# Gated linear attention in a three-part float32 kernel: products on halves of TensorE's array, and another order of VectorE's splits and norms

## The chip, the cores and the metric

The kernel runs on one core of a Trainium2 chip, in one launch. The metric is the device time of that launch in microseconds; the median of three runs of the kernel before is 2018.16 us (2017.99 to 2021.58). TensorE multiplies (PE in the profile, with its weight loads as PEld), VectorE (DVE) and ScalarE (ACT) work on what lies in the on-chip memory SBUF and empty TensorE's banks (PSUM, eight banks `ps` of 512 columns by 128 partitions), GpSimd (POOL) does a few elementwise products, SyncE (SP) issues the DMAs.

## The reference

Input is one sequence of 512 rows by 1024, in float32. Three blocks follow one another: gated linear attention with an MLP, windowed attention with sinks and an MLP, and a block of convolution, dilated attention and a gated feed-forward. The change is mostly in the first:

```python
def gla_mixer(h, w_in, w_gate_up, b_gate_up, g_norm, w_out):
    q, k, v, g, glr = jnp.split(h @ w_in, ...)          # 512, 512, 1024, 1024, 16 columns
    log_a = jax.nn.log_sigmoid(glr @ w_gate_up + b_gate_up) / 16
    # eight chunks of 64 rows, four heads: k 128 wide, v 256 wide
    bc = jnp.cumsum(log_a over a chunk)
    q_dec, k_inv, k_end = q * 128**-0.5 * exp(bc), k * exp(-bc), k * exp(b_last - bc)
    att = tril(q_dec @ k_inv.T)                          # 64 x 64 a chunk and head
    o_intra = att @ v
    dS = k_end.T @ v                                     # 128 x 256 a chunk and head
    S[n + 1] = S[n] * exp(b_last) + dS[n]                # over the chunks
    o = o_intra + q_dec @ S[n]
    o = rms_norm(o over 256, g_norm) * silu(g)
    return o @ w_out
```

Around it: `x = x + rms_norm(m)` and `h = rms_norm(x)` ahead of each MLP.

## The kernel before, in words

Every large matrix product is done in three fp32r products of split operands: high part times high part, high times low, low times high. A weight unit is 1024 columns by 128 partitions (512 KB). SyncE fetches it to one of four raw buffers `WR` (`fetch`, in one order through the kernel), ScalarE copies it rounded to `WH` (`a_cut`), VectorE subtracts to get the low part `WL` (`v_cut`); each of these waits for the buffer's last reader. `product` (L386 to L388) multiplies one unit with 512 columns of activations (`HH`, `HL`), 24 matmuls to a bank; `tokens` (L415 to L417) makes 128 rows of output from up to four units, two banks at a time. Products within an attention are in plain float32. Each engine runs its own list, written out by hand, in order; semaphores marked by name (`k.mark`, `k.on`) tie them, and `k.free[b]` names what frees bank b. `k.ring` sets the banks that products take in turn.

The gated linear attention, TensorE's list in `t_gla`:

- the normed rows are transposed (`t_turn`, L437), then nine projection units `gla_in`: the low-rank tile first (its 16 columns of weights padded to 128), then four of K and four of Q. `t_starts` does the first four, by halves of the rows, while later rows are still being normed. Evacuations are VectorE's (`evac`). After the sixth unit the low-rank result `GLR` (its row 32 is ones, for the bias) is multiplied with `WGU` (L600);
- eight products for V (`tokens`, p = 0 to 7; V's second half is added on VectorE by `evac_v`), and between them the cumulative sums of each head (`decays`, L517) and the transposition of the decayed K (`turn_k`, L526). ScalarE and VectorE work each head's exponentials in `decays(h)`;
- eight gate units `gla_g`, with the attention between them: `scores` (L535) of 128 rows and four heads to bank 3, which VectorE masks to `DG` with a block-diagonal mask; `intra` (L547) for two chunks in one product of 128 x 128; then chunk by chunk `chunk(n)`: the inter-chunk product with the state (L560, 64 columns), and the new state's product (L569, on 64 rows of the array, banks 7 and 4), which VectorE adds to the decayed state `ST` (L1732). ScalarE takes the output of two chunks from banks 5 and 6 (`outs`);
- the norm: squares by ScalarE, sums by TensorE with a matrix of ones (`o_sums`, L583; rows 0 to 255 after the sixth gate unit, both through bank 3), logarithm and exponential by ScalarE (`o_norm`), eight scalings by VectorE (L1742), times the gates on GpSimd (L2167), and `o_cut` splits the result to `HH`, `HL` (L1098, L1748), which the gate units have read until then;
- the output product `t_ends`, row tile by row tile, with the second half's sums between its first two parts. `a_ends` and `v_ends` then make mean, scale, sum, mean and normed row `MT` for each row tile, which `t_turn` transposes for the MLP.

The windowed attention (`t_swa`) runs eight pairs of heads: `score` (L682, each head on 64 rows of the array), `turn` (transposed weights, L697), `out` (product with V, L711), with projection units between, and `ahead` does parts of the output product for row tile 0 in the last two pairs. Its tail has its own order on VectorE (`early=True` in `v_ends`).

## Time and profile before

| what | us |
|---|---|
| median of three runs | 2018.16 |
| the profiled execution | 2019.09 |
| its span | 2017.3 |
| TensorE busy (matmul) | 1987.8 |
| TensorE weight loads | 1638.9 |
| VectorE busy | 1187.9 |
| ScalarE busy | 853.9 |
| GpSimd busy | 28.4 |

The span is that of the core's first to last instruction. A matmul in float32 stands in the trace as two records, one in fp32r as one. Matmuls are pipelined, so a record's duration is longer than the distance to the next record's start; prices are best read from start to start. Of the chain that ended last, TensorE holds 92%. All of the gated linear attention lies in the first 264 us of the span, the windowed attention with its tail between 589 and 779 us.

### The profile page before, as it was taken

How to read it: one execution, taken by the hardware profiler on the slowest of the kernel's cores; microseconds unless marked ns; L12 is line 12 of the kernel's file. 1: busy time of each engine (PE TensorE's matmuls, PEld its weight loads, DVE VectorE, ACT ScalarE, POOL GpSimd, SP SyncE). 2: the span in 40 equal slices, each digit the busy share in tenths (PEclk: the TensorE clock that was granted, in tenths of full speed). 3: DMA queues.
4: the chain of work that ended last, by engine and by line, in shares of the span. 5: the costliest groups of instructions: out<-in, count | busy, mean ns of one | idle time of the engine just before them, and what ended most of it. 6: DMA issues, size and time to landing. Idle time of an engine off the chain costs nothing.

```text
span 2017.3 us, 25047 instructions
## 1 busy us (share of the span) xinstructions
PE 1987.8 (99%) x9784; PEld 1638.9 (81%) x9784; DVE 1187.9 (59%) x1776; ACT 853.9 (42%) x1374; POOL 28.4 (1%) x34
## 2 busy tenths in 40 slices
PE   7999999999999999999999999999999999999999
PEld 7788898888888778888888987667788888888887
DVE  4344564444456756444445686777798647774764
ACT  4533544233335744423233426667634324442431
POOL 0001100000000000000000000000000000000000
PEclk9999999999999999999999999999999999999999
DMA  5131123223323113322323232222232313222321
GB/s 193 53 125 42 63 94 103 96 84 127 98 89 147 53 53 93 96 96 92 125 89 99 95 95 94 84 77 81 74 97 86 126 68 104 96 95 84 115 94 63
DMA packets 51857, 188.53 MB, mean 93 GB/s; under 512 B 5755, under 2 KB 6011, under 8 KB 51100
## 3 DMA queue, kind: packets, MB, share of 16 engines
q1 hardware_dynamic: 51740, 186.92, 28.1%
q8 instruction: 79, 1.29, 0.3%
q14 instruction: 38, 0.31, 0.1%
HBM read 184.80 MB, written 2.10 MB: 93 GB/s over the span
## 4 chain that ended last, share of the span: by engine, by line
PE 92%; DVE 3%; ACT 3%; issue 1%; DMA 0%; SPq 0%; DVEq 0%; ACTq 0%
PE ps L386 18%; PE ps L388 18%; PE ps L387 17%; PE ps L415 10%; PE ps L417 10%; PE ps L416 10%; DVE WL L1566 1%; PE ps L813 1%; PE ps L437 1%; PE ps L785 1%; PE ps L799 1%; PE ps L569 1%; PE ps L560 1%; PE ps L711 1%; PE ps L763 1%
## 5 line engine op out<-in xcount | busy, mean ns | idle before, releaser
L386 PE MATMUL ps<-HH,WH 128*128 128x512 f32 (+1 forms) x1784 | 667.2, 374 | 3.0 <-DVE HL L1593 1.7
L388 PE MATMUL ps<-HH,WL 128*128 128x512 f32 (+1 forms) x1784 | 655.5, 367 | 0.0
L387 PE MATMUL ps<-HL,WH 128*128 128x512 f32 (+1 forms) x1784 | 655.0, 367 | 0.0
L954 ACT ACTIVATE WH<-WR 128x1024 fp32r<-128x1024 f32 x305 | 320.6, 1058 | 622.8 <-PE ps L388 347.5
L1566 DVE TENSOR_TENSOR WL<-WR,WH 128x1024 fp32r<-128x1024 f32 x305 | 372.5, 1226 | 196.8 <-ACT WH L954 190.1
L386 PEld LDWEIGHTS ps<-HH,WH 128*128 128x128 f32 x1784 | 337.3, 189 | 71.9 <-issue 16.1
L388 PEld LDWEIGHTS ps<-HH,WL 128*128 128x128 f32 x1784 | 337.1, 189 | 55.8
L387 PEld LDWEIGHTS ps<-HL,WH 128*128 128x128 f32 x1784 | 337.7, 189 | 54.1 <-issue 1.9
L415 PE MATMUL ps<-WH,HIDH 128*128 128x512 f32 x624 | 243.4, 390 | 0.0
L417 PE MATMUL ps<-WL,HIDH 128*128 128x512 f32 x624 | 243.1, 390 | 0.0
L416 PE MATMUL ps<-WH,HIDL 128*128 128x512 f32 x624 | 243.0, 389 | 0.0
L1919 DVE SCALAR_TENSOR_TENSOR M<-AP,PAR,M 128x512 f32<-128x512 f32 x240 | 167.2, 757 | 0.3 <-ACT M L1274 0.3
L415 PEld LDWEIGHTS ps<-WH,HIDH 128*128 128x128 f32 x624 | 117.2, 188 | 24.8 <-DVE WL L1566 0.6
L416 PEld LDWEIGHTS ps<-WH,HIDL 128*128 128x128 f32 x624 | 117.2, 188 | 24.2
L417 PEld LDWEIGHTS ps<-WL,HIDH 128*128 128x128 f32 x624 | 117.2, 188 | 24.2
L1605 DVE TENSOR_TENSOR MT<-ps,MT 128x1024 f32<-128x1024 f32 x52 | 63.6, 1222 | 114.0 <-PE ps L417 114.0
L1815 DVE TENSOR_TENSOR HIDL<-RT,HIDH 128x512 fp32r<-128x512 f32 x64 | 44.3, 693 | 87.2 <-ACT HIDH L1164 87.2
L1160 ACT ACTIVATE RT<-RT 128x512 f32<-128x512 f32 x64 | 40.5, 632 | 121.1 <-DVE RT L1813 121.1
L2120 DVE COPY UP<-ps 128x512 f32<-128x512 f32 x44 | 30.4, 692 | 67.1 <-PE ps L388 67.1
L2133 DVE TENSOR_TENSOR X<-ps,X 128x1024 f32<-128x1024 f32 x24 | 29.4, 1223 | 53.0 <-PE ps L417 53.0
L415 PE MATMUL ps<-WH,HH 128*128 128x512 f32 x128 | 51.6, 403 | 1.2 <-DVE WL L1566 1.2
L1593 DVE TENSOR_TENSOR HL<-ps,HH 128x512 fp32r<-128x512 f32 x48 | 30.9, 685 | 33.6 <-ACT HH L974 33.6
(227 smaller groups left out, 2075.1 us busy)
## 6 DMA issues: line engine op xcount, KB each, us to landing
WR<-in_up SPq DMA_DIRECT2D x108, 512.0 KB, 3.6
WR<-in_down SPq DMA_DIRECT2D x86, 512.0 KB, 3.5
WR<-in_in SPq DMA_DIRECT2D x56, 512.0 KB, 3.6
WR<-in_swa_in SPq DMA_DIRECT2D x10, 512.0 KB, 4.3
WR<-in_gla_in SPq DMA_DIRECT2D x9, 512.0 KB, 6.6
WR<-in_gla_v SPq DMA_DIRECT2D x8, 512.0 KB, 3.5
WR<-in_gla_g SPq DMA_DIRECT2D x8, 512.0 KB, 4.7
GAIN<-in_gain SPq DMA_DIRECT2D x4, 1024.0 KB, 7.1
```

What stands on the lines that cost most here:

```text
L386: e.matmul(ps, wh, hi[:, c, cols], start=c == 0, stop=False)
L387: e.matmul(ps, wh, lo[:, c, cols], start=False, stop=False)
L388: y = e.matmul(ps, wl, hi[:, c, cols], start=False, stop=c == x.n - 1)
L415: e.matmul(m.ps[b + f], xh, x.wh[:, w], start=first, stop=False)
L416: e.matmul(m.ps[b + f], xl, x.wh[:, w], start=False, stop=False)
L417: y = e.matmul(m.ps[b + f], xh, x.wl[:, w], start=False, stop=last)
L954: e.activation(x.wh[:, 0:n], m.WR[:, u % RAW, 0:n], AF.Copy).then_inc(*k.mark("whi", u))
L1160: e.activation(buf, buf, AF.Square).then_inc(*k.mark("sqr", u))
L1566: e.tensor_tensor(x.wl[:, 0:n], m.WR[:, u % RAW, 0:n], x.wh[:, 0:n].bitcast(F32), A.subtract).then_inc(*k.mark("wlo", u))
L1605: e.tensor_tensor(out, p, out, A.add).then_inc(*k.mark("mv", *key))
L1815: e.tensor_tensor(m.HIDL[:, i % 16, :], buf, m.HIDH[:, i % 16, :].bitcast(F32), A.subtract).then_inc(*k.mark("hid", layer, i))
L1919: e.scalar_tensor_tensor(m.M[:, c, :], m.AP[:, c, t:t + T], par(m, "conv_w", c * 31 + t, 1), m.M[:, c, :], A.mult, A.add).then_inc(*k.mark ...
```

## The change

- Low-rank tile: it moves behind the four units of K. Its low weights are written by VectorE into columns 32 to 47 of each slice of the high ones, so that two products in place of three give both parts, in rows 0 to 15 and 32 to 47; `GLR` has 64 rows, `WGU` holds its weights twice, and the bias comes by adding a column of the identity.
- Scores: all four pairs of chunks at once, after the first gate unit, each chunk and head as 64 x 64 on one half of the array's columns, to banks 2 and 3; two maskings by VectorE into `ATT` (which lies where `BC` was, so the DMA of the gains waits for the last `intra`).
- `intra` chunk by chunk on the two halves of the array's rows, chunk 2t to bank 5 and 2t + 1 to bank 6; `states` for both chunks of a pair together, on row halves, to banks 2, 3 and 4, 7; `inter` alone. ScalarE takes each chunk's output (`outs(n)`). The last gate unit is cut after five of eight slices, and the last pair's work stands in the gap.
- The norm: VectorE adds the squares in pairs, sums are one product of 512 columns a pair of heads, in two banks; the first half's scaling moves to the eighth gate unit's step and stands ahead of the last state update on VectorE.
- The low part of the first gate unit is made within the last head's `decays`. V's products take their banks in the other order, gate units use two banks.
- Windowed attention: the first scores come after half a projection unit; `ahead` does three slices, then one. In its tail VectorE norms row tile 1 before it splits tile 0, and one weight split goes behind the evacuation of row tile 3. In the last block's `evac_y` a weight split moves ahead of the low part.

The diff, cut to what is spoken of:

```diff
-    m.GLR = over("GLR", [33, T], gains)
-    m.WGU = over("WGU", [33, T], gains + 2 * KB)
+    m.GLR = over("GLR", [64, T], gains)
+    m.WGU = over("WGU", [64, T], gains + 2 * KB)
     m.BC = over("BC", [128, 2, T], gains + 4 * KB)
+    m.ATT = over("ATT", [128, 4, 4, 64], gains + 4 * KB)
+GLA_O = (5, 6)
+GLA_DS = ((2, 3), (4, 7))
@@ t_gla
+    def low_rank(j):
+        x, b = k.units[u + j], k.bank()
+        e.wait_ge(*k.on("wlo", u + j))
+        e.wait_ge(*k.on(*k.free[b]))
+        for c in range(8):
+            w = x.wh[:, c * 128:(c + 1) * 128]
+            e.matmul(ps[b], w, hi[:, c, :], start=c == 0, stop=False)
+            y = e.matmul(ps[b], w, lo[:, c, :], start=False, stop=c == 7)
+        y.then_inc(*k.mark("unit", u + j))
+        k.free[b] = ("ev", u + j)
+        k.value["bank", u + j] = b
+    def scores():
+        for t in range(4):
+            b = 2 + t // 2
+            if t % 2 == 0:
+                e.wait_ge(*k.on(*k.free[b]))
+            for h in range(4):
+                f = (t % 2 * 4 + h) * 64
+                for s in range(2):
+                    sl = slice(t * 128 + 64 * s, t * 128 + 64 * s + 64)
+                    x = e.matmul(ps[b][64 * s:64 * s + 64, f:f + 64], m.KI[:, h, sl], m.Q[:, h, sl], start=True,
+                                 stop=True)
+            if t % 2:
+                x.then_inc(*k.mark("att", t // 2))
+                k.free[b] = ("mask", t // 2)
+        e.wait_ge(*k.on("mask", t // 2))
+        for s in range(2):
+                col = (2 * h + f) * 64
+                for s in range(2):
+                    rows, last = slice(64 * s, 64 * s + 64), h == 3 and f == 1
+                    x = e.matmul(ps[GLA_O[s]][:, col:col + 64], m.V[rows, t, h * 256 + f * 128:h * 256 + f * 128 + 128],
+                                 m.ATT[rows, t, h, :], start=h == 0 and f == 0, stop=last and t == 0 and s == 0,
+                                 skip_group_check=True)
+                    if last:
+                        x.then_inc(*k.mark("intra", 2 * t + s))
...
+    def inter(n):
+        b = GLA_O[n % 2]
+        e.wait_ge(*k.on("st", n - 1, 3))
+        for h in range(4):
+            for f in range(2):
+                col = (2 * h + f) * 64
+                x = e.matmul(ps[b][:, col:col + 64], m.ST[:, h, f * 128:(f + 1) * 128], m.Q[:, h, n * 64:n * 64 + 64],
+                             start=False, stop=h == 3 and f == 1, skip_group_check=True)
+        x.then_inc(*k.mark("inter", n))
+        k.free[b] = ("o", n)
+    def states(t):
+        for h in range(4):
+            for s in range(2 if t < 3 else 1):
+                rows, b = slice(64 * s, 64 * s + 64), GLA_DS[s][h // 2]
+                if h % 2 == 0:
+                    e.wait_ge(*k.on("ke", 3))
+                    e.wait_ge(*k.on(*k.free[b]))
+                x = e.matmul(ps[b][:, h % 2 * 256:h % 2 * 256 + 256], m.KET[rows, h, t, :],
+                             m.V[rows, t, h * 256:(h + 1) * 256], start=True, stop=True)
+                if h % 2:
+                    x.then_inc(*k.mark("ds", 2 * t + s, h // 2))
+                    k.free[b] = ("st", 2 * t + s, h)
...
-        for pair, b in ((0, 6), (1, 7)) if i else ((0, 3), (1, 3)):
-            e.wait_ge(*k.on("osq", i, 4 * pair + 3))
+        for pair, b in ((0, 6), (1, 7)) if i else ((0, 2), (1, 3)):
+            e.wait_ge(*k.on("opair", i, pair))
             e.wait_ge(*k.on(*k.free[b]))
-            for h in range(2):
-                for f in range(2):
-                    x = e.matmul(ps[b][:, 256 * h:256 * h + 256], cst(m, "ones"), sq[:, 4 * pair + 2 * h + f, :],
-                                 start=f == 0, stop=f == 1)
-            x.then_inc(*k.mark("osums", i, pair))
+            e.matmul(ps[b].rearrange("p (h t) -> p h t", h=2), cst(m, "ones"), sq[:, 4 * pair:4 * pair + 4:2, :], start=True,
+                     stop=True).then_inc(*k.mark("osums", i, pair))
             k.free[b] = ("oln", i, pair)
...
-    k.ring(0, 1, 2, 3)
-    for j in range(4, 9):
+    k.ring(2, 3, 0, 1)
+    low_rank(4)
+    for j in range(5, 9):
...
-    k.ring(0, 1, 2, begin=2)
-    for j in range(8):
+    k.ring(0, 1)
+    for j in range(7):
         product(e, k, g + j, hi, lo, 2, k.bank(), ev="ae")
         if j == 0:
-            scores(0)
+            scores()
         elif j % 2:
             intra(j // 2)
-            chunk(j - 1)
+            if j > 1:
+                inter(j - 1)
+            states(j // 2)
         else:
-            chunk(j - 1)
-            scores(j // 2)
-        if j == 5:
+            inter(j - 1)
+        if j == 6:
             o_sums(0)
-    chunk(7)
+    b = k.bank()
+    product(e, k, g + 7, hi, lo, 2, b, ev="ae", c1=5)
+    intra(3)
+    inter(6)
+    states(3)
+    product(e, k, g + 7, hi, lo, 2, b, ev="ae", c0=5)
+    inter(7)
     t_ends(e, k, k.at["gla_out"], hi, lo, 0, "mlp0", "sc", lambda t: lambda c: [("hlo", "o", t // 2, c)], lambda: o_sums(1))
@@ t_swa
-    def ahead(c, f):
+    def ahead(c, n, f):
-        tokens(e, k, w + c, 2, m.WOH, m.WOL, c, 0, 0, None, lambda c: [("wol", c)], c == 0, False, (f,))
+        tokens(e, k, w + c, n, m.WOH, m.WOL, c, 0, 0, None, lambda c: [("wol", c)], c == 0, False, (f,))
     for p in range(8):
-        score(p)
+        if p:
+            score(p)
         if p >= 2:
             out(p - 2)
         if p < 6:
             product(e, k, u + 4 + p, m.HH, m.HL, 2, 0, ev="ae", c1=4)
+            if p == 0:
+                score(p)
             if p >= 1:
                 turn(2 * p - 2)
             product(e, k, u + 4 + p, m.HH, m.HL, 2, 0, ev="ae", c0=4)
-                ahead(0, 0)
+                ahead(0, 2, 0)
             turn(2 * p - 2)
-            ahead(2 if p == 6 else 0, p - 6)
+            if p == 6:
+                ahead(2, 1, 0)
+            else:
+                ahead(3, 1, 0)
+                ahead(0, 2, 1)
             turn(2 * p - 1)
             if p == 7:
-                ahead(2, 1)
+                ahead(2, 2, 1)
@@ a_gla, decays(h) and the loop over gate tiles
         e.wait_ge(*k.on("dec0", h))
         e.activation(DEC[:, h, :], bcv[:, :, 63], AF.Exp).then_inc(*k.mark("dec", h))
+        if h == 3:
+            a_cut(e, k, v + 8)
         e.wait_ge(*k.on("qd", "e", h))
         e.activation(e3, e3, AF.Exp).then_inc(*k.mark("dec3", h))
+    def outs(n):
+        e.wait_ge(*(k.on("inter", n) if n else k.on("intra", 0)))
+        e.activation(m.M[:, :, n * 64:(n + 1) * 64], ps[GLA_O[n % 2]].rearrange("p (f c) -> p f c", f=8),
+                     AF.Copy).then_inc(*k.mark("o", n))
-        if j % 2 == 0 and j:
-            outs(j // 2 - 1)
+        if j > 1:
+            outs(j - 2)
         if j == 5:
             o_squares(0)
+        if j == 7:
             o_norm(0)
     w = k.at["gla_out"]
+    outs(6)
     evac_g(7)
     for c in range(8):
         o_cut(0, c)
         if c == 1:
             a_cut(e, k, w + 3)
-    outs(3)
+    outs(7)
     o_squares(1)
@@ v_cut
-        e.tensor_tensor(x.wl[:, 0:n], m.WR[:, u % RAW, 0:n], x.wh[:, 0:n].bitcast(F32), A.subtract).then_inc(
-            *k.mark("wlo", u))
+        if u == k.at["gla_in"] + 4:
+            raw, wh = m.WR[:, u % RAW, :].rearrange("p (c f) -> p c f", c=8), x.wh.rearrange("p (c f) -> p c f", c=8)
+            e.tensor_tensor(wh[:, :, 32:48], raw[:, :, 0:16], wh[:, :, 0:16].bitcast(F32), A.subtract).then_inc(
+                *k.mark("wlo", u))
+        else:
+            e.tensor_tensor(x.wl[:, 0:n], m.WR[:, u % RAW, 0:n], x.wh[:, 0:n].bitcast(F32), A.subtract).then_inc(
+                *k.mark("wlo", u))
@@ v_ends
         v_normed(e, k, tag, 0)
         middle(1)
         head(2)
+        v_normed(e, k, tag, 1)
         v_split(e, k, tag, 0)
-        v_normed(e, k, tag, 1)
         middle(2)
         v_cut(e, k, following)
         v_normed(e, k, tag, 2)
         v_split(e, k, tag, 1)
-        v_cut(e, k, following + 2)
+        v_cut(e, k, following + 1)
     head(3)
+    v_cut(e, k, following + 2)
     v_split(e, k, tag, 2)
     middle(3)
     v_cut(e, k, following + 3)
@@ v_gla
-        if j == 0:
-            e.wait_ge(*k.on("pads0"))
-            e.tensor_copy(m.GLR[0:32, :], p[0:32, :]).then_inc(*k.mark("ev", u + j))
-        elif j <= 4:
-            e.tensor_copy(m.KI[:, j - 1, :], p).then_inc(*k.mark("ev", u + j))
+        if j < 4:
+            e.tensor_copy(m.KI[:, j, :], p).then_inc(*k.mark("ev", u + j))
+        elif j == 4:
+            e.wait_ge(*k.on("const"))
+            e.tensor_scalar(m.GLR[:, :], p[0:64, :], cst(m, "ident")[0:64, 16:17], None, A.add).then_inc(*k.mark("ev", u + j))
         e.tensor_tensor(e3v, bcv[:, :, 63:64].broadcast_to((128, 8, 64)), bcv, A.subtract).then_inc(*k.mark("qd", "e", h))
+        if h == 3:
+            v_cut(e, k, v + 8)
         e.wait_ge(*k.on("dec3", h))
         e.tensor_tensor(e3, e3, m.KI[:, h, :], A.mult).then_inc(*k.mark("kend", h))
+    def masks(i):
+        e.wait_ge(*k.on("att", i))
         e.wait_ge(*k.on("late"))
+        e.wait_ge(*k.on("dec3", 3))
+        e.tensor_tensor(m.ATT[:, 2 * i:2 * i + 2, :, :].rearrange("p t h c -> p (t h) c"),
+                        ps[2 + i].rearrange("p (h c) -> p h c", h=8), mask, A.mult).then_inc(*k.mark("mask", i))
+    def add_squares(i):
+        sq = m.LA[:, :, :].rearrange("p a (b t) -> p (a b) t", b=2)
+        for pair in range(2):
+            c = 4 * pair
+            e.wait_ge(*k.on("osq", i, c + 3))
+            e.tensor_tensor(sq[:, c:c + 4:2, :], sq[:, c:c + 4:2, :], sq[:, c + 1:c + 4:2, :], A.add).then_inc(
+                *k.mark("opair", i, pair))
         if j == 0:
-            scores(0)
-        elif j % 2:
+            masks(0)
+            masks(1)
+        if j == 6:
+            add_squares(0)
+        if j == 7:
+            o_norm(0)
+        if j:
             chunk(j - 1)
-        else:
-            chunk(j - 1)
-            scores(j // 2)
-        if j == 5:
-            o_norm(0)
     w = k.at["gla_out"]
     for c in range(8):
         o_cut(0, c)
         if c == 3:
             v_cut(e, k, w + 3)
+    add_squares(1)
     v_cut(e, k, w + 7)
     o_norm(1)
@@ v_second, evac_y(j)
         e.tensor_tensor(tmp, tmp, m.GB[:, j, :], A.add).then_inc(*k.mark("y", j))
+        if 3 <= j < 7:
+            v_cut(e, k, u0 + j + 4)
         e.wait_ge(*k.on("hhi", "y", j))
         e.tensor_tensor(m.HL[:, j, :], tmp, m.HH[:, j, :].bitcast(F32), A.subtract).then_inc(*k.mark("hlo", "y", j))
-            v_cut(e, k, u + 6)
-        elif 3 <= j < 7:
-            v_cut(e, k, u + j + 4)
+            v_cut(e, k, u0 + 6)
@@ sync_program
-    fetch(e, k, at["gla_out"] - 1)
-    e.wait_ge(*k.on("z", 3))
-    gains("mlp0", 1, ("qd", "k", 3))
+    fetch(e, k, at["gla_out"] + 3)
+    gains("mlp0", 1, ("intra", 7))
     fetch(e, k, at["down02"] - 1)
```

## Rows read from the trace of the kernel before

**Rows 1.** Page, busy time of an engine (share of the span) and its instructions.
```profile
PE 1987.8 (99%) x9784; PEld 1638.9 (81%) x9784; DVE 1187.9 (59%) x1776; ACT 853.9 (42%) x1374; POOL 28.4 (1%) x34
```
**Rows 2.** Windows by stage: stretch, length, busy of PE, PEld, DVE, ACT, POOL; granted clock; DMA.
```profile
125.35:172.67 47.32, 47.32 (x257) 40.16 (x257) 17.06 (x26) 11.77 (x19) 0.00 (x0) 1.00 0.32 112
172.67:222.94 50.27, 48.44 (x259) 41.17 (x258) 24.35 (x39) 26.06 (x47) 6.65 (x8) 0.97 0.20 63
...
212.80:216.20 3.40, 3.40 (x9) 2.60 (x8) 1.67 (x5) 3.37 (x10) 0.00 (x0) 0.51 0.50 157
```
**Rows 3.** Timeline: start us, us, instruction, [idle before]; a projection tile's first and last record.
```profile
43.11 0.40 PE L386 MATMUL ps<-HH,WH 128*128 128x512 f32 x1
...
48.35 0.39 PE L388 MATMUL ps<-HH,WL 128*128 128x512 f32 x1
```
**Rows 4.** Timeline of TensorE, second and third gate tile and what follows each.
```profile
131.74 0.48 PE L386 MATMUL ps<-HH,WH 128*128 128x512 f32 x1
...
137.28 1.95 PE L547 MATMUL ps<-DG,V 128*128 128x128 f32 x16
139.15 1.99 PE L569 MATMUL ps<-V,KET 64*128 64x256 f32 x8
141.07 0.50 PE L386 MATMUL ps<-HH,WH 128*128 128x512 f32 x1
...
146.66 1.89 PE L560 MATMUL ps<-Q,ST 128*128 128x64 f32 x16
148.48 1.99 PE L569 MATMUL ps<-V,KET 64*128 64x256 f32 x8
150.41 1.16 PE L535 MATMUL ps<-Q,KI 128*128 128x128 f32 x8
```
**Rows 5.** Timeline of VectorE and TensorE ahead of the first gate tile.
```profile
122.95 1.22 DVE L1708 TENSOR_TENSOR V<-ps,V 128x1024 f32<-128x1024 f32 x1
...
125.35 0.50 PE L386 MATMUL ps<-HH,WH 128*128 128x512 f32 x1 [0.99 <-DVE WL L1566]
```
**Rows 6.** Timeline of TensorE in the second block's attention: scores, then product with V.
```profile
1235.91 1.57 PE L785 MATMUL ps<-K,Q 64*128 64x128 f32 x12
1237.41 0.50 PE L386 MATMUL ps<-HH,WH 128*128 128x512 f32 x1
...
1271.53 0.27 PE L813 MATMUL ps<-PT,V 128*64 128x128 f32 x1
...
1271.64 0.27 PE L813 MATMUL ps<-PT,V 128*64 128x128 f32 x1
```
**Rows 7.** Timeline of TensorE from the norm's first sums to its second.
```profile
186.63 1.97 PE L583 MATMUL ps<-LA,CONST 128*128 128x256 f32 x8 [0.87 <-ACT ACC L1089]
...
210.71 2.00 PE L560 MATMUL ps<-Q,ST 128*128 128x64 f32 x16 [0.96 <-DVE ST L1732]
212.51 0.48 PE L415 MATMUL ps<-WH,HH 128*128 128x512 f32 x1
...
219.67 3.62 PE L583 MATMUL ps<-LA,CONST 128*128 128x256 f32 x16
```
**Rows 8.** Timeline from ScalarE's mean of row tile 0 to its transposition.
```profile
234.25 1.03 ACT L963 ACTIVATE HL<-ps 128x1024 fp32r<-128x1024 f32 x1 [0.17 <-PE ps L417]
...
241.49 1.28 DVE L1584 SCALAR_TENSOR_TENSOR MT<-X,SMALL,GAIN 128x1024 f32<-128x1024 f32 x1
...
244.94 1.04 PE L437 MATMUL ps<-CONST,MT 128*128 128x128 f32 x8
```
**Rows 9.** Timeline of TensorE: its waits in the windowed attention and its tail.
```profile
642.83 1.14 PE L682 MATMUL ps<-WK,WQ 64*128 64x256 f32 x8 [0.58 <-ACT WQ L1207]
...
709.25 0.50 PE L415 MATMUL ps<-WH,WOH 128*128 128x512 f32 x1 [1.65 <-DVE WL L1566]
...
760.59 0.33 PE L437 MATMUL ps<-CONST,MT 128*128 128x128 f32 x1 [1.50 <-DVE MT L1584]
...
778.19 0.33 PE L437 MATMUL ps<-CONST,MT 128*128 128x128 f32 x1 [1.43 <-DVE MT L1584]
```

More of the change, by code:

```diff
@@ L528, in turn_k @@
         k.free[6] = ("ke", h)
-    def scores(t):
-        sl = slice(t * 128, (t + 1) * 128)
-        e.wait_ge(*k.on("qd", "k", 3))
-        e.wait_ge(*k.on(*k.free[3]))
-        for h in range(4):
-            x = e.matmul(ps[3][:, h * 128:(h + 1) * 128], m.KI[:, h, sl], m.Q[:, h, sl], start=True, stop=True)
-        x.then_inc(*k.mark("att", t))
-        k.free[3] = ("mask", t)
+    def low_rank(j):
[9 more added lines that the diff above has]
+        k.value["bank", u + j] = b
@@ L550, in intra @@
-        x.then_inc(*k.mark("intra", t))
-    def chunk(n):
-        t, half = n // 2, n % 2
-        rows = slice(64 * half, 64 * half + 64)
-        if n:
-            e.wait_ge(*k.on("st", n - 1, 3))
-            for h in range(4):
-                for f in range(2):
-                    col = (h % 2 * 2 + f) * 128 + 64 * half
-                    x = e.matmul(ps[5 + h // 2][:, col:col + 64], m.ST[:, h, f * 128:(f + 1) * 128],
-                                 m.Q[:, h, n * 64:n * 64 + 64], start=False, stop=half == 1, skip_group_check=True)
-            x.then_inc(*k.mark("inter", n))
-        if n < 7:
-            for pair, b in ((0, 7), (1, 4)):
-                e.wait_ge(*k.on("ke", 3))
-                e.wait_ge(*k.on(*k.free[b]))
-                for f in range(2):
-                    h = 2 * pair + f
-                    x = e.matmul(ps[b][:, f * 256:(f + 1) * 256], m.KET[rows, h, t, :],
-                                 m.V[rows, t, h * 256:(h + 1) * 256], start=True, stop=True)
-                x.then_inc(*k.mark("ds", n, pair))
-                k.free[b] = ("st", n, 2 * pair + 1)
-        if half:
-            k.free[5], k.free[6] = ("o", t, 0), ("o", t, 1)
+                col = (2 * h + f) * 64
@@ L599, in t_gla @@
                     e.wait_ge(*k.on(*k.free[4 + t]))
-                e.matmul(ps[4 + t][:, :], m.GLR[0:33, tile(t)], m.WGU[0:33, :], start=True,
+                e.matmul(ps[4 + t][:, :], m.GLR[:, tile(t)], m.WGU[:, :], start=True,
                          stop=True).then_inc(*k.mark("z", t))
@@ L1082, in o_norm @@
         for pair in range(2):
[L1083 removed]
+            b = 6 + pair if i else 2 + pair
             e.wait_ge(*k.on("osums", i, pair))
@@ L1722, in chunk @@
             return
-        for pair, b in ((0, 7), (1, 4)):
+        for pair in range(2):
+            b = GLA_DS[n % 2][pair]
             for f in range(2):
```

54 lines of the change are left out of this document (17 added, 37 removed).

## The prediction

> **What bounds the kernel.** I read the engines' busy line first: TensorE has work for 1987.8 of 2017.3 us [rows 1]. So the end moves by what TensorE's own list gets shorter, and by those of its few stalls that go; work of VectorE and ScalarE counts only where TensorE waits for it. Then the windows by stage [rows 2]: 47.32 us from the first gate tile (125.35) to the sixth (172.67), 50.27 from there to the second part of the output product (222.94). The other edits lie in the windowed attention and its tail (626 to 779 us), and one in the last block's output. The profiled execution took 2019.09 us, 1.8 more than its span and 0.9 more than the median of 2018.16; I subtract from the median.
>
> **Unit prices.** A record is one MATMUL row of the trace; a product in float32 makes two, a product in fp32r one. 128x512 in fp32r: (48.35 - 43.11) / 23 = 0.228 us from start to start [rows 3]. A whole gate tile (24 records): 5.54 to 5.59 [rows 4], call it 5.6. Old intra-chunk product of two chunks: 1.87; states of one chunk (8 records, 64 rows of the array, 256 columns): 1.93; inter-chunk product (16 records, 64 columns): 1.82. That is 0.11 a record, as much as the intra product's records of 128 columns take (0.12): the weight load is what it waits for [rows 4].
>
> **Low-rank tile.** Three products a slice become two: 16 records in place of 24, -8 x 0.228 = -1.8 us. The split of its weights shrinks too, on VectorE. The gate product that needs the result comes a whole tile (5.4 us) later, and the copy, split and evacuation before it (1.1 + 1.2 + 0.7) sum to 3; no stall. Its K of 33 becomes 64: 512 columns either way, 0.
>
> **First gate tile.** It waits 0.99 until 125.35 for its low part, split last on VectorE [rows 5]. The change puts that split ahead of the last decay's work. But the tile now takes bank 0, free only after the evacuation of V's third part, which ran at 122.95 for 1.22; the split (1.2) now stands before it, less the wait for ScalarE that it fills: it ends near 124.9. So -0.4 (0 to -1.2), and the bank is the new releaser.
>
> **Do half-array products overlap?** The edit lives on this. In attention scores, pairs on the two 64-row halves make 12 records of 128, 256 and 384 columns in 1.50 us (1235.91 to 1237.41); one after another their columns alone are 12 records at 0.11, 0.21 and 0.32, 2.6 us [rows 6]. Those are full pairs with a weight load of 128 columns each, and the load overlaps too. Column halves (64 output partitions) run in pairs as well: a pair per 0.11 us at 128 columns (1271.53, 1271.64). What no row has is 64 columns on halves.
> - Intra: 8 pairs x 2 records x 0.11 (load-bound as the inter product is) = 1.8 per two chunks, old 1.78 to 1.88: nothing gained. If the loads did not overlap, 32 records at 0.11 = 3.6, +7.2 in all.
> - States: 4 pairs x 2 x 0.216 = 1.7 for two chunks in place of 3.86; the last tile has one chunk. 4 x 1.7 = 6.9 against 7 x 1.73 = 12.1 without seams: -5.2.
> - Scores: 16 pairs x 2 x 0.055 = 1.8, old 3.5. The bound above is all 64 records singly, 3.6. I take 1.8, since column pairs ran at the price of one. The old scores: 32 records of 128 columns at 0.11.
> - Seams: each excursion to a half-array form and back costs 0.1 before it, an unhidden first load of 0.1, and the same on leaving, 0.4 (148.48's eight records took 1.93 where 8 x 0.216 is 1.73, with another 0.2 at the neighbours). Seven before; eight after (scores; chunk pair 0 in one; three pairs with the inter product between intra and states).
>
> Here the Trainium skill speaks against the change: "TensorEngine Tiling (Array Packing)", section Tiling Modes, says that changing the mode drains the engine. The trace agrees in kind, and its price is the 0.4 above. The same page's section Performance Considerations warns that a small free dimension gains nothing from tiling, for about 60 cycles go with each matmul; by it (an estimate: 60 cycles at 2.4 GHz are 25 ns) the scores' 64 records take 1.6 us, under my 1.8, so it changes nothing unless the pairs' loads serialize.
>
> **Stage 125.35 to 172.67, summed anew.** Five gate tiles 28.0; scores 2.2 with seam; intra and states of the first pair 3.9; inter 1.8; second pair (intra 1.8, inter 1.8, states 1.7, seams 0.7) 6.0; inter 1.8: 43.7. That is -3.6 (-1.4 if scores run singly and seams cost more).
>
> **Stage 172.67 to 222.94.** Besides columns it holds stalls [rows 7]: the norm's sums wait for one shared bank (0.87 at 186.63); the last inter product waits for the state, 0.96 at 210.71, with 8.4 us of load-bound work since the last gate tile; and right behind it the granted clock shows 0.51 in the stretch 212.80 to 216.20 [rows 2], the lower of TensorE's two levels (1.2 of 2.4 GHz). There 24 records take 7.16 us (212.51 to 219.67) where 5.5 is usual: 1.6 lost. The sums are 16 + 16 records at 0.214, 7.7 us with the stall; after the change VectorE adds the squares in pairs and 4 records of 512 columns (0.43 each) do each half: 1.75. The stretch anew: three gate tiles and one cut 16.9; pair three 6.0; inter 1.8; sums 1.75; pair four 6.0; last inter 1.8; output part 5.5; sums 1.75: 41.5. That is -8.8. It assumes that the clock stays up: the run of such work before the output product falls from 8.4 to 1.8 us, and the longest left is 6. The update of the last state now stands behind the norm's eight scalings on VectorE (6.1 us beside GpSimd, after two table loads on ScalarE); I place its end at 31.9 us after the sixth gate tile's start and TensorE's need at 32.2. Only 0.3 covers it; if the cover goes, each us late is one lost.
>
> **What is late next.** The high parts of the first half all need the last gate tile, which now ends 1.8 us before the output product and not 8.4 before. ScalarE works them off, then squares, four splits and the second norm, so its first mean starts some 14.5 us after the second output part's start, old 11.3 (234.25 against 222.94). From that mean to the first normed row are 8.5 us, and its transposition stood at 244.94, with 2.1 us to spare [rows 8]. 14.5 + 8.5 = 23.1 against TensorE's 21.8: +1.4 stall (0 to 3). The gains' DMA (1 MB) moves behind the fourth output tile's fetch and behind the last intra product; the output product's last four fetches queue behind that wait on SP and are wanted some 13 us after it: 0.
>
> **Windowed attention.** Three parts [rows 9].
> - The first scores go behind a half tile: their 0.58 stall goes. But VectorE and ScalarE start 1.75 us later, and ScalarE's evacuation of that tile stands behind two heads' exponentials, so the next tile starts 0.5 later: +0.5.
> - At 709.25 the output's fourth slice waits 1.65 for its low part; it moves to the next step. The second slice's transposition and pair 7 come earlier, then the product with V waits for copies of head 13 that ScalarE issues behind exponentials. Of 1.8, I keep 1.3.
> - In the tail VectorE norms row tile 1 before it splits tile 0: the 1.50 at 760.59 goes. The row update of tile 3 comes one split (1.1) earlier, and the 1.43 at 778.19 grows by the rest, since VectorE's chain leads there. It ends 1.35 earlier in all.
> Together -2.1 (0 to -3.5). The output's reordered splits in the last block: TensorE waits there for a bank that VectorE frees, not for a split, so 0.
>
> **Sum.** -1.8 - 0.4 - 3.6 - 8.8 + 1.4 - 2.1 = -15.3; 2018.2 - 15.3 = 2002.9 us.
>
> **Rivals.**
> - Loads on halves serialize at 64 columns: intra +7.2, scores +1.8, 2012. For: no row with 64 columns on halves. Against: both kinds of halves run in pairs [rows 6]. Chance 0.06.
> - The ends follow VectorE and ScalarE: the state update late by 1, the stall before the first transposition 3, attention gives nothing: 2002.9 + 1.0 + 1.6 + 2.1 = 2007.6. For: covers of 0.3 and a queue that I set out by hand. 0.15.
> - The change doesn't do what it says with the clock: it falls once all the same, +1.6, 2004.5; inside my band. 0.08.
> - Slower: the clock takes half-array work for idling. A drop like that of 212.8 costs 1.6; to be slower by 0.2% (4 us) there must be (15.3 + 4) / 1.6 = 12 such drops in the 85 us of the stage; if all of it ran at the lower level, +40, 2043. For: the one drop follows sparse work. Against: the same work at 137 to 150 us ran at full rate [rows 4]. 0.01.
> - The forecast, 2000.5 to 2006: 0.70.
>
> Range 1999.5 to 2009.5: it leaves out the serial loads and what lies below. Within 0.2% (4 us, about what can be told apart) means above 2014: serial loads and late ends together, 0.02; slower 0.01; faster 0.97.
>
> **What would show it.** Low-rank: 16 records on a line of their own. First gate tile: starts 0.4 earlier behind VectorE's V. States: start pairs under 10 ns apart and 1.7 a pair of chunks. Scores: 1.8. No clock drop between the sixth gate tile and the transpositions. A new stall of 1 to 2 us before the first transposition. At the windowed attention the gaps of 1.65 and 1.50 gone, the last one larger. It would be wrong if intra records stand 0.11 apart singly, or if the last inter product waits by more than a microsecond for the state.

## The result and the profile after

The changed kernel takes 2003.37 us (median of four; 2002.37 to 2003.88), the kernel before 2019.87 (median of 2017.99, 2018.16, 2021.58 and 2025.02; the first three are those known ahead of the prediction): a ratio of 0.9914 (95% interval 0.9893 to 0.9934). A later comparison, nine executions of the kernel before and five of the changed one, gave 2018.24 and 2003.03, 0.9922 (0.9908 to 0.9935). The forecast was 2002.9, range 1999.5 to 2009.5.

The page of the kernel after, busy line (see [rows 1]): TensorE 12.4 us shorter, and the same share of the span.

```profile
PE 1975.4 (99%) x9848; PEld 1626.4 (81%) x9848; DVE 1187.3 (59%) x1777; ACT 854.3 (43%) x1374; POOL 28.6 (1%) x34
```

Windows of the kernel after: stretch, length, busy time of PE, PEld, DVE, ACT and POOL, granted clock, DMA share, GB/s. The second and third answer the two of [rows 2], the fourth is the way from the second output part to the first transposition, the last two are the windowed attention (from its fifth projection tile) and its tail.

```profile
44.52:48.18 3.66, 3.66 (x19) 3.02 (x17) 2.13 (x3) 1.06 (x1) 0.00 (x0) 1.00 0.59 152
124.60:167.73 43.13, 43.13 (x328) 36.23 (x329) 15.21 (x22) 11.38 (x16) 0.00 (x0) 1.00 0.28 90
167.73:208.72 40.99, 40.86 (x258) 33.28 (x258) 23.63 (x41) 23.09 (x45) 6.77 (x8) 1.00 0.21 78
208.72:232.03 23.31, 22.34 (x99) 18.01 (x97) 18.12 (x26) 15.84 (x27) 7.02 (x8) 1.00 0.26 91
613.52:738.68 125.16, 123.04 (x783) 99.21 (x782) 79.74 (x281) 77.60 (x216) 0.00 (x0) 1.00 0.24 85
738.68:763.53 24.85, 23.48 (x154) 20.89 (x152) 21.82 (x26) 13.98 (x26) 0.00 (x0) 1.00 0.28 85
```

47.32 us became 43.13, 50.27 became 40.99, with the clock at 1.00 where [rows 2] had 0.97 and a stretch of 0.51. Against that 22.00 us (222.94 to 244.94 of before) became 23.31. The windowed attention with its tail went from 152.71 (626.33 to 779.04) to 150.01. Between the two stages little moved: 18.9 us became 19.0 from the first transposition to the MLP's first product, then it is 362.49 in both kernels, and behind the tail 1238.3 and 1238.4. One thing isn't the change's: the first 48 projection records of the program took 7.14 us in the profiled run of before and 8.46 in that of after. They are the same records in every kernel here, and took 7.1 to 8.5: they start 0.21 apart and later 0.12, and the step comes at 18.2 us in before and at 21.3 in after. That is why the spans differ by 15.4 only, where the other stretches give some 17; so I compare experiments by stretches, not by spans.

Timeline of TensorE after: start us, us, instruction, [idle before]. It answers [rows 4] and [rows 7].

```profile
124.60 0.47 PE L389 MATMUL ps<-HH,WH 128*128 128x512 f32 x1 [0.63 <-DVE V L1764]
...
130.26 2.08 PE L559 MATMUL ps<-Q,KI 128*64 128x64 f32 x64
132.27 0.50 PE L389 MATMUL ps<-HH,WH 128*128 128x512 f32 x1
...
137.94 2.00 PE L576 MATMUL ps<-ATT,V 64*128 64x64 f32 x32
139.77 1.95 PE L603 MATMUL ps<-V,KET 64*128 64x256 f32 x16
141.65 0.50 PE L389 MATMUL ps<-HH,WH 128*128 128x512 f32 x1
...
186.53 1.94 PE L614 MATMUL ps<-LA,CONST 128*128 128x512 f32 x4
187.90 0.79 PE L389 MATMUL ps<-HH,WH 128*128 128x512 f32 x1
...
199.83 1.89 PE L590 MATMUL ps<-Q,ST 128*128 128x64 f32 x16
201.85 0.47 PE L418 MATMUL ps<-WH,HH 128*128 128x512 f32 x1
...
232.03 0.33 PE L440 MATMUL ps<-CONST,MT 128*128 128x128 f32 x1 [0.97 <-DVE MT L1637]
```

From start to start: the scores' 64 records take 2.01 us, intra and states of the first pair of chunks 1.83 + 1.88, the norm's sums 1.37. The states cost 1.9 for two chunks where [rows 4] had 1.9 for one. No wait stands before the last inter product any more; from its start to the output part it is 2.02 us, though, where such a product takes 1.7, and the trace names no releaser for those 0.3. A new wait, 0.97, stands before the first transposition.

### The profile page after: what moved, and what is told of

It reads as the page before. It is cut to its first block, busy times and chain, and to the rows that moved or that the text cites. A ratio compares the mean times of both kernels' runs of the same rounds, so it can differ in the third digit from the quotient of the medians.

```text
span 2001.9 us, 25170 instructions
## 1 busy us (share of the span) xinstructions
PE 1975.4 (99%) x9848; PEld 1626.4 (81%) x9848; DVE 1187.3 (59%) x1777; ACT 854.3 (43%) x1374; POOL 28.6 (1%) x34
## 4 chain that ended last, share of the span: by engine, by line
PE 92%; ACT 4%; DVE 3%; issue 1%; DMA 0%; POOL 0%; SPq 0%; ACTq 0%; DVEq 0%; POOLq 0%
PE ps L389 18%; PE ps L391 18%; PE ps L390 18%; PE ps L418 10%; PE ps L419 10%; PE ps L420 10%; PE ps L858 1%; PE ps L440 1%; PE ps L830 1%; PE ps L844 1%; PE ps L808 1%; PE ps L749 1%; PE ps L735 1%; PE ps L590 1%; PE ps L720 1%
```

## The experiments

Each is the changed kernel with one edit, unless it is said otherwise; numbers of the changed kernel are those of the profile above. Each of these was executed once, but for the last two. Stretches that an edit doesn't touch agree within 0.1 us between all these traces, so times by stretches can be compared; how often the clock falls, one execution can't show.

**States, intra and scores with the halves in turn.** The same records, but first those of one half of the array, then those of the other. The first:

```diff
-        for h in range(4):
-            for s in range(2 if t < 3 else 1):
+        for s in range(2 if t < 3 else 1):
+            for h in range(4):
```

> The changed kernel with the same 28 state products, but all four heads of the even chunk before those of the odd one, so that no two neighbours lie on different row halves. My theory (halves run side by side, each pair at the price of one): 16 records in a row instead of 8 pairs, so each of the three pairs of chunks takes 16 x 0.216 = 3.5 in place of the 1.9 that its states take now, +1.7 each, +5.1 us between the first gate tile and the second output part; the fourth pair has one chunk and stays. Rival (the stage got shorter by fewer waits and seams, not by overlap): 0.

```diff
-        for h in range(4):
-            for f in range(2):
-                col = (2 * h + f) * 64
-                for s in range(2):
+        for s in range(2):
+            for h in range(4):
+                for f in range(2):
+                    col = (2 * h + f) * 64
```

> The changed kernel with the 64 intra products ordered by row half: eight of the even chunk, then eight of the odd one, in each pair of chunks. My theory: a pair costs one 128-column weight load now (0.11 us a pair of records); in turn 32 records x 0.11 = 3.5 in place of 1.9, +1.7 for each of four pairs, +6.8 us. If only the products overlapped and the weight loads did not, the changed kernel would stand at 3.5 already: 0. The run of sparse work grows to 7.7 us in the third and fourth pair; if the clock falls there, 1.6 more for each fall.

```diff
-            for h in range(4):
-                f = (t % 2 * 4 + h) * 64
-                for s in range(2):
+            for s in range(2):
+                for h in range(4):
+                    f = (t % 2 * 4 + h) * 64
```

> The changed kernel with the 32 score products ordered by column half within each 128 rows: four heads of the even chunk, then four of the odd one. The scores take 2.01 us now for 64 records. My theory (column halves run side by side at 64 columns): 64 records x 0.055 = 3.5 + seam 0.2, so +1.7 us. Rival (at 64 columns a record is bound by its issue, not by its load or its columns, so order is nothing): 0.

Measured: 2005.86, 2018.10 and 2003.18 us, and by stretches +2.9, +14.7 and +0.6. None is the number expected. Timeline of TensorE, states in turn; windows of line 603 alone in it (length, records under way on PE, on PEld, clock); then the scores in turn:

```profile
158.73 2.96 PE L603 MATMUL ps<-V,KET 64*128 64x256 f32 x16
161.62 0.50 PE L389 MATMUL ps<-HH,WH 128*128 128x512 f32 x1
```

```profile
158.70:159.69 0.99, 0.96 (x4) 0.85 (x5) 1.00 0.00 0
159.69:160.40 0.71, 0.71 (x8) 0.70 (x7) 1.00 0.00 0
160.40:161.40 1.00, 1.00 (x8) 0.77 (x5) 1.00 0.00 0
```

```profile
129.12 2.69 PE L559 MATMUL ps<-Q,KI 128*64 128x64 f32 x64
131.74 0.50 PE L389 MATMUL ps<-HH,WH 128*128 128x512 f32 x1
```

Sixteen records of 256 columns singly would be 16 x 0.216 = 3.5 us; they took 2.89 with a seam of 0.2, that is 12.5 pitches (a pitch is the time from one record's start to the next). The windows show where the rest is: four records begin in the first 0.99 us, seven in the 0.71 around the middle (of the eight under way one began earlier), and five in the last 1.00 (three of the eight began earlier). Around the middle, where one half's records end and the other's begin, they run side by side: the other half's first record starts at 159.70, when three of the first half's eight haven't started yet. So halves in turn do overlap, but only as far as the engine reaches ahead, about three records. The scores fit: 8 groups of 8 meet at 7 seams, 64 - 7 x 3 = 43 pitches of 0.058 are 2.5, and 2.62 was measured against 2.01. That halves run side by side is shown for all three products; my price for undoing it was too high by this reach (three times 0.96 in place of 1.7 for the states).

The intra product went the other way. Timeline and windows of the kernel with intra in turn (all engines):

```profile
156.03 3.39 PE L576 MATMUL ps<-ATT,V 64*128 64x64 f32 x32
159.35 2.12 PE L590 MATMUL ps<-Q,ST 128*128 128x64 f32 x16
161.40 3.51 PE L603 MATMUL ps<-V,KET 64*128 64x256 f32 x16
164.84 0.50 PE L389 MATMUL ps<-HH,WH 128*128 128x512 f32 x1
```

```profile
161.00:164.40 3.40, 3.40 (x18) 2.77 (x18) 0.88 (x2) 0.60 (x1) 0.00 (x0) 0.51 0.00 0
181.40:188.20 6.80, 6.80 (x33) 5.52 (x32) 0.95 (x3) 0.60 (x1) 0.00 (x0) 0.51 0.00 0
205.30:215.50 10.20, 10.20 (x32) 8.01 (x31) 3.45 (x7) 2.91 (x5) 2.55 (x4) 0.51 0.64 251
124.65:216.64 91.99, 91.99 (x557) 77.11 (x557) 33.79 (x53) 27.96 (x44) 6.74 (x8) 0.89 0.20 71
```

The product itself costs 3.32 for 1.93, four times 1.39 = 5.5 us (29 pitches of 0.11: the reach of three again). The other 9.2 us of the 14.7 (91.99 against 77.25 from the first gate tile to the output product) are the clock: three falls to the lower of the two levels, 1.2 GHz, 20.4 us in all. Each comes 0.5 to 1.7 us behind the 3.3 us of an intra product in turn, during the inter product that follows it. The first intra product in turn took 3.2 us too, but the states follow it and no inter product, and it brought none; nor did states or scores in turn. Ten traced executions of kernels with the intra side by side and the last gate tile cut show no fall in this stage. So of the three orders only that of the intra bears on the clock here: an item that my sum put down as "nothing gained".

**The last gate tile whole.**

```diff
-    product(e, k, g + 7, hi, lo, 2, b, ev="ae", c1=5)
+    product(e, k, g + 7, hi, lo, 2, b, ev="ae")
...
-    product(e, k, g + 7, hi, lo, 2, b, ev="ae", c0=5)
```

> The changed kernel with the last gate tile in one piece ahead of the fourth pair's intra, inter and state products. From that tile to the output product there are then some 8.6 us of load-bound work with a wait of 0.9 for the last state (its update follows the norm's scalings). Theory A (it is the run of sparse work before the output product that lets the granted clock fall): one fall, 1.6 us lost in the output product's first part; the wait +0.4 net; and the stall of 0.97 before the first transposition goes, since the gate tile ends 6 us before and ScalarE's queue is done earlier: +1.0 in all. Rival B (the clock fell before for its idle time in front of the sums, which is gone): no fall, 0.4 - 1.0 = -0.6.

**The kernel before, with the cut alone.**

```diff
-        product(e, k, g + j, hi, lo, 2, k.bank(), ev="ae")
+        b = k.bank()
+        product(e, k, g + j, hi, lo, 2, b, ev="ae", c1=5 if j == 7 else None)
...
+    product(e, k, g + 7, hi, lo, 2, b, ev="ae", c0=5)
```

> The kernel before, with one edit of the change alone: the last gate tile is cut after five of its eight slices, and the rest stands behind the last state update. Theory (the cut is what kept the clock up and hid the wait for the state): in the stretch before the second output part the wait of 0.96 us and the 1.6 us lost to the clock go, and the granted clock shows no fall there; against that a stall of 1 to 1.5 us comes up ahead of the first transposition, as in the changed kernel. From the sixth gate tile to the second output part 50.3 becomes 47.7 to 47.9; from there to the first transposition 22.0 becomes 23.1 to 23.5; net -1.0 to -1.5. Rival (the columns saved on halves kept the clock up, not the cut): the clock falls all the same, 49.3 for the first stretch. Rival 2 (the cut is free at the tail, the stall there comes from the other edits): 22.0 stays.

Measured: 2005.02 and 2017.48 us. Windows of the first (sixth gate tile to second output part, the stretch of the fall, then to the transposition) and its timeline; then the same of the second:

```profile
166.29:211.19 44.90, 43.93 (x259) 35.98 (x258) 27.36 (x44) 26.68 (x49) 6.77 (x8) 0.92 0.23 82
199.40:206.20 6.80, 6.80 (x25) 6.03 (x26) 4.99 (x11) 6.23 (x18) 0.32 (x1) 0.50 0.71 263
211.19:233.36 22.17, 22.17 (x98) 18.14 (x97) 16.61 (x25) 12.51 (x23) 7.01 (x8) 1.00 0.19 74
```

```profile
199.26 3.55 PE L590 MATMUL ps<-Q,ST 128*128 128x64 f32 x16 [0.97 <-DVE ST L1794]
```

```profile
173.27:221.27 48.00, 46.99 (x259) 40.10 (x258) 22.34 (x37) 23.29 (x45) 6.67 (x8) 1.00 0.14 45
221.27:243.27 22.00, 22.00 (x99) 18.14 (x98) 16.78 (x26) 14.38 (x25) 7.01 (x8) 1.00 0.28 96
```

Without the cut the wait for the state is back at 0.97 and the clock falls for 6.8 us, twice as long as in [rows 2]: 44.90 for 40.99, +3.9, of which 1.0 is the wait and 3.0 the clock (1.28 in the inter product, 1.75 in the output part). The tail gets back 1.14. I had put the fall at its old length, so the net is +2.8 where I had 1.0.

With the cut alone, in the old kernel, neither wait nor fall is there: 50.27 becomes 48.00 (-2.3). For the wait that is shown. For the clock this run alone proves little, since the kernel before has the fall in some executions only: of nine in the later comparison, six have a mean granted clock of 1.000 (2017.91 to 2018.37 us), two 0.999 (2019.13 and 2019.39) and one 0.998 (2022.16), and a fall of 3.4 us to half rate by itself brings the mean to 0.9992. Against the six, 2017.48 is 0.4 to 0.9 less: the wait, and no 1.6. That the cut keeps the clock up in the changed kernel rests on one execution without it, which has the fall, and the ten traced with it, which have none; "twice as long" lies within what the kernel before does from one execution to the next.

The tail of the old kernel with the cut stays at 22.00: the stall that I expected there doesn't come. From the last gate record to the second output part there are 18.8 us in the kernel before, 10.8 with the cut alone and 8.9 in the changed kernel; only the last is too short. The stall takes the cut and the rest of the change together; which part of the rest was not tried.

**ScalarE's squares in two instructions.**

```diff
-        for c in range(8):
+        for c in range(0, 8, 4):
...
-            e.activation(sq[:, c, :], m.M[:, c, HALF[i]], AF.Square).then_inc(*k.mark("osq", i, c))
+            e.activation(sq[:, c:c + 4, :], m.M[:, c:c + 4, HALF[i]], AF.Square).then_inc(*k.mark("osq", i, c + 3))
```

> The changed kernel; the norm's squares on ScalarE in two instructions of 1024 elements a row in place of eight of 256, for each half. Theory (ScalarE's queue sets the stall of 0.97 us ahead of the first transposition): each of eight instructions costs a fixed part of some 0.2 us beside its elements, the queue before the first mean gets 0.5 to 1.2 us shorter, and the stretch from the second output part to the first transposition goes from 23.3 to 22.3 to 22.8. Rival (VectorE's pairwise sums and splits set it, and now wait for four squares at a time): 23.3 or up to 0.5 more.

Window of this kernel and its first transposition:

```profile
207.82:230.57 22.75, 22.33 (x98) 18.00 (x96) 17.57 (x26) 15.30 (x26) 7.00 (x8) 1.00 0.27 94
```

```profile
230.57 0.33 PE L440 MATMUL ps<-CONST,MT 128*128 128x128 f32 x1 [0.42 <-DVE MT L1637]
```

ScalarE is 0.54 us less busy (six instructions fewer, 0.09 each and not the 0.2 expected), and the stall falls by 0.55 of its 0.97: this queue sets it. What follows the squares in it isn't ScalarE's own. Timeline of ScalarE in the changed kernel:

```profile
213.50 1.28 ACT L1139 ACT_TABLE_LOAD   x1
...
222.25 0.42 ACT L1144 ACTIVATE HH<-M 128x256 fp32r<-128x256 f32 x1 [0.46 <-POOL M L2231]
223.14 0.42 ACT L1144 ACTIVATE HH<-M 128x256 fp32r<-128x256 f32 x1 [0.47 <-POOL M L2231]
223.46 1.01 ACT L1008 ACTIVATE HL<-ps 128x1024 fp32r<-128x1024 f32 x1
```

Each of the second half's high parts waits 0.46 for GpSimd's product, so GpSimd's eight scalings seem to stand in the chain too; no run changes them. The first mean begins 14.7 us after the second output part.

**The windowed attention: evacuation first.** In the first step the projection tile is evacuated before the two heads' exponentials.

```diff
+        if p == 0:
+            evac(4)
...
-        if p < 6:
+        if 0 < p < 6:
```

> The changed kernel; in the windowed attention's first step ScalarE evacuates the projection tile before the two heads' exponentials. Theory (what is taken from one waiter is given to the next): the stall of 1.35 us before the sixth projection tile goes, but the transposition of the step and the product with V wait later by as much, since their copies stand behind the later exponentials; from the fifth projection tile to the tail's start 125.2 us becomes 124.6 to 125.2. Rival (the order on ScalarE at that place is the whole loss): 123.8 to 123.9.

**First scores in their old place.**

```diff
-        if p:
-            score(p)
+        score(p)
...
-            if p == 0:
-                score(p)
```

> The changed kernel with the windowed attention's first scores back ahead of the projection's half tile. Theory (they cost 0.5 to 0.6 where they are now, since exponentials and evacuation on ScalarE start 1.75 us later and the next tile waits for the evacuation): a stall of 0.58 us before the scores returns, the 1.35 before the sixth tile falls under 0.2; from the fifth to the sixth projection tile 25.6 us becomes 25.0; the sum of the attention falls by 0.6. Rival (the later place was a gain that my model of the queue lost): 25.6 or more.

Where TensorE waits in the changed kernel, with evacuation first, and with the scores back (timelines); and the window from the fifth to the sixth projection tile with the scores back:

```profile
639.09 0.47 PE L389 MATMUL ps<-HH,WH 128*128 128x512 f32 x1 [1.35 <-ACT WQ L1255]
```

```profile
644.63 0.96 PE L735 MATMUL ps<-CONST,PW 128*128 128x128 f32 x7 [0.59 <-ACT PTW L1267]
```

```profile
629.71 1.13 PE L720 MATMUL ps<-WK,WQ 64*128 64x256 f32 x8 [0.58 <-ACT WQ L1252]
```

```profile
613.20:638.15 24.95, 24.37 (x183) 21.84 (x181) 12.55 (x40) 15.26 (x34) 0.00 (x0) 1.00 0.55 203
```

Evacuation first: the 1.35 goes, 0.59 stands before the next transposition, and the first product with V takes 2.4 for 1.7. By 649.7 it is 36.31 us from the fifth tile, 36.12 in the changed kernel: all given back and a little more (150.18 to the tail's end), so the theory of the waiters holds. Scores back: 24.95 against 25.57, and 149.47 against 150.01 to the tail's end. So the later place of the first scores costs 0.55; the change loses there.

**The slices ahead, and the tail's order, as before.**

```diff
-            if p == 6:
-                ahead(2, 1, 0)
-            else:
-                ahead(3, 1, 0)
-                ahead(0, 2, 1)
+            ahead(2 if p == 6 else 0, 2, p - 6)
```

> The changed kernel with the first slices of the output product ahead as in the kernel before. Theory (the slice waited for its low part, and its move is what saved 1.3): the wait of 1.65 us comes back in place of 0.37, and the stretch of the windowed attention from the fifth projection tile to the tail gets longer by 1.3 to 1.7. Rival (the shorter wait comes from the earlier scores and not from the order of the slices): 0 to 0.4.

```diff
-        v_normed(e, k, tag, 1)
...
+        v_normed(e, k, tag, 1)
...
-        v_cut(e, k, following + 1)
+        v_cut(e, k, following + 2)
```

> The changed kernel with VectorE's order in the tail of the attention as before (row tile 0 split before row tile 1 is normed). Theory: the wait inside the output product ahead of the tail's transposition comes back at 1.50 for 0.38, the one before the next product grows from 0.98 to 1.43, and the tail gets longer by 1.35 to 1.6. Rival (VectorE's total work sets the end, and its order moves nothing): 0 to 0.3.

Windows of the whole windowed attention with its tail, first kernel, then second (the changed kernel's is 150.01), each with its waits, and last the waits in the changed kernel's tail:

```profile
613.35:765.01 151.66, 146.89 (x935) 120.09 (x934) 101.68 (x306) 91.65 (x242) 0.00 (x0) 1.00 0.25 84
```

```profile
696.83 0.50 PE L418 MATMUL ps<-WH,WOH 128*128 128x512 f32 x1 [1.65 <-DVE WL L1615]
```

```profile
612.40:764.24 151.84, 146.74 (x936) 120.01 (x934) 101.58 (x306) 91.56 (x242) 0.00 (x0) 1.00 0.24 84
```

```profile
745.54 0.33 PE L440 MATMUL ps<-CONST,MT 128*128 128x128 f32 x1 [1.48 <-DVE MT L1637]
...
763.39 0.33 PE L440 MATMUL ps<-CONST,MT 128*128 128x128 f32 x1 [1.44 <-DVE MT L1637]
```

```profile
751.90 1.16 PE L440 MATMUL ps<-CONST,MT 128*128 128x128 f32 x8 [0.38 <-DVE HL L1646]
...
762.68 1.09 PE L440 MATMUL ps<-CONST,MT 128*128 128x128 f32 x8 [0.98 <-DVE MT L1637]
```

+1.65 and +1.83. The waits of [rows 9] are back in size, so each edit works alone and by its own mechanism. The second is above the 1.35 to 1.6 expected: I had set the 1.50 against the 0.38, but they stand before different transpositions. The first has no wait at all in the changed kernel, the second has the 0.38, and at the third 0.98 goes back to 1.44.

**Both repairs.** The changed kernel with the first scores in their old place and the squares in two instructions, timed beside the changed kernel itself.

> The changed kernel itself, for the comparison with the next. 2003.4 us within 1; against the kernel before 0.991 to 0.993.

> The changed kernel with both repairs: first scores of the windowed attention back in their old place, and the norm's squares in two instructions a half. Theory (the two stalls are independent, 0.55 each): the sum falls by 1.1, to 0.9945 of nothing but its own stretches: second output part to first transposition 22.75, fifth to sixth projection tile of the attention 24.95; median 1.1 below the changed kernel's, 2002.3. Rival (one stall's gain is taken by the next wait in line): 0.5 or less.

(The words "to 0.9945 of nothing" in that text are a slip; it has no ratio.) Measured, on one chip: 2001.98 us (2001.46 to 2002.06) against 2003.03 (2002.52 to 2003.67); the two don't overlap, and 1.05 is the 1.1 expected. Against the kernel before, 2018.24: 0.9916 (0.9902 to 0.9929). Windows of the kernel with both repairs, where the changed kernel has 23.28 and 150.00:

```profile
207.63:230.37 22.74, 22.33 (x98) 18.00 (x96) 17.55 (x26) 15.27 (x26) 7.02 (x8) 1.00 0.27 94
...
611.84:761.32 149.48, 146.76 (x936) 120.23 (x934) 101.57 (x306) 91.90 (x242) 0.00 (x0) 1.00 0.24 85
```

The two stalls are independent. This is the fastest version of the study.

## Why the prediction was right, step by step

- **Low rank** -1.8: the 16 records take 3.66 us, 0.228 each; exact.
- **First gate tile** -0.4: it starts 0.36 earlier against the stage ahead, and the new releaser is VectorE's V, the bank, as named.
- **Stage to the sixth gate tile** -3.6: measured -4.2. Every item came out a little shorter: scores with their seam 2.0 (2.2), first pair 3.7 (3.9), a later pair with its inter product 5.8 (6.0), an inter product 1.7 (1.8). The states' records start in pairs 7 ns apart, as said. The term that was mis-sized is the seam: 0.4 per excursion, where scores and first pair show 0.14 and 0.19 beyond their pitches (1.87 and 3.52) and 0.1 in the tile behind.
- **Stage to the second output part** -8.8: measured -9.3 against the profiled execution of before, which has the fall. The sums took 1.37 and 1.32 in place of 1.75, for the four records' last columns run under what follows. The state update ended 31.8 us after the sixth gate tile's start (31.9 forecast), TensorE wanted it at 32.1 (32.2). No wait, and no fall of the clock; that the cut removes the wait is shown by both runs on it, for the clock it rests on what is said there.
- **First transposition** +1.4: measured +1.3, first mean at +14.7 for 14.5. The size was right with some luck: 14.5 + 8.5 is 23.0 and not 23.1, and against the old stretch of 22.0 that gives +1.0. The 1.4 came from setting it against 21.8, where TensorE's own work takes 22.2 (22.17 with the whole tile, without a stall; 0.2 of it are the sums' last columns, which the stage before no longer holds); the stall itself is 0.97. That the queue ahead of the mean sets it is shown by the squares (-0.55 when they shrink); GpSimd's products in that queue, which the sum doesn't name, are read from the timeline only.
- **Windowed attention** -2.1: measured -2.7. First scores +0.6 for +0.5 (shown by their return); the slices ahead are worth 1.65, I kept 1.3 of them, too careful about copies behind exponentials (a wait of 0.36 stands there); the tail is 1.6 shorter for 1.35. One sign failed: the last wait, 1.43 at 778.19, should have grown and fell to 0.98, so VectorE's chain didn't lead there in the way I had it.
- **0 elsewhere**: 0.0 between the stages, 0.1 behind the tail.

By these stretches the change gave 17.1 us, and I had 15.3. The six terms are each within 0.6, and the errors add up, since all that count are to the careful side.

That the forecast came so near the median is in part luck. The sum subtracts 1.6 for the fall of the clock from a median of 2018.2, and an execution of before at 2018.2 has no such fall (six of nine, see the last gate tile). There the change can save 17.1 - 1.6 = 15.5, and 15.2 was measured in that comparison. So 1.6 too much for the clock and 1.8 too little in the other terms cancel. The 16.5 of the first comparison has a reference midway between 2018.16 and 2021.58.

The first rival (loads on halves serialize) didn't come about: 32 pairs of the scores take 2.01 us against 3.5 before. The Trainium skill's warning in "TensorEngine Tiling (Array Packing)", section Performance Considerations, is against splitting a dimension that is small already. At the scores' 64 columns it didn't bite: 1.87 without the seam against 3.5. The prediction's estimate from that section's 60 cycles, 1.6, lies under the 1.87.

One argument fell nevertheless. The last rival had the clock take half-array work for idling, at 0.01 and with "the same work at 137 to 150 us ran at full rate" against it. For work side by side that holds, and the changed kernel has no fall. But the order bears on it: with the intra in turn the same records lost 9.2 us to the clock in the one execution. The argument had looked at what is computed and not at the order in which it is issued. Had the two loops stood the other way round, the forecast would have been 15.2 us below that execution's 2018.10, out of its range.

It stays open why the states in turn bring no fall and the intra product in turn does, how often either kernel would fall in more executions, and what the 0.1 us behind the tail is.

## What to carry to other kernels

Give the two halves of the array their records in alternation, from the innermost loop: the engine overlaps halves only a few records ahead. After a change that thins out TensorE's work, look at the granted clock and not at the busy share, and keep a piece of a large product to run behind the small ones: here three slices of a product kept behind them were worth 2.8 us in the execution that was traced. Before a loss to the clock goes into a sum, look whether the median execution has it. And where a stretch gets shorter, ask which queue had its slack in it.

## What the runs showed of the hardware that I had not expected

- Records of one half of the array start while about three earlier ones of the other half are still queued: 16 records on halves in turn take 2.89 us, alternated 1.93, and 3.5 would be the serial price (an estimate, 16 x 0.216).
- A record of 64 columns with 64 weight columns comes every 0.058 us, half the 0.11 of one with 128 weight columns and 64 columns (2.62 us for the scores in turn, with a seam of 0.14 and 43 pitches; 1.82 for 16): with the same 64 columns to multiply, the pitch goes with the weight columns loaded.
- The granted clock fell for 3.4, 6.8 and 10.2 us in one kernel, 6.8 in another and 3.4 in the kernel before, and TensorE was busy throughout those stretches. One and the same kernel, the one before, went without a fall in six of nine executions.
- The program's first 48 records took 7.1 to 8.5 us in kernels that don't differ there. That is more than the two repairs together, so single spans can't show them. What sets it was not tried.
